# Modulation slices inside the wide stage, sums between products, first two wide chunks side by side

## The reference

```python
for l in range(DEPTH):                                   # DEPTH = 2
    mod_l = silu(c) @ w_mod[l] + b_mod[l]                # six vectors of 1024: sh1, sc1, g1, sh2, sc2, g2
    mod_c = silu(c_ctx) @ w_mod[l] + b_mod[l]            # the same for the context tokens
    y_l, y_c = token_mixer(modulate(rms_norm(x)), ...)   # retention, GLA, GQA, differential attention
    x = x + g1 * y_l
    x = x + g2 * conv_ffn(modulate(rms_norm(x, norm2[l]), sh2, sc2), w_up[l], conv_w[l], conv_b[l], w_down[l])
    # in layer 0 also for the context tokens

def conv_ffn(h, w_up, conv_w, conv_b, w_down):
    u = h @ w_up                                          # 1024 -> 2 x 2816
    a = depthwise_conv(u[..., :D_FF], conv_w, conv_b)     # width 3
    return (silu(a) * u[..., D_FF:]) @ w_down
```

## Time and profile before

| what | value |
|---|---|
| three timed runs | 2981.74, 2987.41, 2996.21 us; median 2987.41 us |
| the profiled execution | 2991.67 us, its span 2989.9 us |
| PE busy | 2731.8 us (91%) |
| POOL, DVE, ACT busy | 1522.0 us (51%), 1342.2 us (45%), 669.0 us (22%) |
| mean granted TensorE clock | 0.945 |
| DMA | 277.84 MB, mean 93 GB/s |
| wide stage of layer 0 | about 1142 to 1549 us |
| wide stage of layer 1 | from 2605 us |

### The profile page before, as it was taken

How to read it: one execution, slowest core, us unless ns; L and a number is a source line. 1 busy time by engine, 2 the same in 40 slices (tenths; PEclk the granted TensorE clock), 3 DMA queues, 4 the chain that set the end, 5 groups by cost and what they waited for, 6 DMA issues and landing times.

```text
span 2989.9 us, 37995 instructions
## 1 busy us (share of the span) xinstructions
PE 2731.8 (91%) x15620; PEld 2221.8 (74%) x15620; DVE 1342.2 (45%) x1756; ACT 669.0 (22%) x1130; POOL 1522.0 (51%) x1412
## 2 busy tenths in 40 slices
PE   5899989999988998999989997998889887899999
PEld 2688877777766886888877886786667666688877
DVE  4522066643566826555562135216643677421221
ACT  4211132221144511110020003013212245211110
POOL 2443447522412542565568524565834425488886
PEclk8899989999989998999989998999989898999999
DMA  7422412311311821333433362221212116333322
GB/s 244 134 66 89 116 31 62 87 38 50 106 38 40 256 72 57 113 113 113 121 103 111 91 205 55 83 68 49 65 50 61 46 36 208 88 92 98 94 89 80
DMA packets 361592, 277.84 MB, mean 93 GB/s; under 512 B 10139, under 2 KB 322111, under 8 KB 360908
## 3 DMA queue, kind: packets, MB, share of 16 engines
q1 hardware_dynamic: 359040, 272.57, 30.7%
q10 hardware_dynamic: 1612, 2.75, 0.2%
q0 software_dynamic: 768, 0.09, 0.0%
HBM read 246.01 MB, written 29.36 MB: 92 GB/s over the span
## 4 chain that ended last, share of the span: by engine, by line
PE 79%; DVE 11%; ACT 4%; POOL 3%; DMA 2%; issue 2%; SPq 0%; DVEq 0%; ACTq 0%; POOLq 0%
PE ps L445 18%; PE ps L446 17%; PE ps L447 17%; PE ps L664 4%; PE ps L990 3%; PE ps L595 2%; PE ps L484 2%; PE ps L486 2%; PE ps L485 2%; POOL w_hi L1127 1%; PE ps L684 1%; POOL w_lo L1130 1%; PE ps L626 1%; DVE arena L1695 1%; PE ps L791 1%
## 5 line engine op out<-in xcount | busy, mean ns | idle before, releaser
L1127 POOL TENSOR_TENSOR w_hi<-ring,tiny 128x512 fp32r<-128x512 f32 x516 | 592.2, 1148 | 1196.9 <-PE ps L447 659.5
L445 PE MATMUL ps<-hh,w_hi 128*128 128x512 f32 (+1 forms) x2272 | 852.6, 375 | 45.1 <-DVE hl L1665 24.7
L1130 POOL TENSOR_TENSOR w_lo<-ring,w_hi 128x512 fp32r<-128x512 f32 (+1 forms) x572 | 790.1, 1382 | 104.8 <-ACT w_hi L1291 64.4
L446 PE MATMUL ps<-hl,w_hi 128*128 128x512 f32 (+1 forms) x2272 | 826.2, 364 | 0.0
L447 PE MATMUL ps<-hh,w_lo 128*128 128x512 f32 (+1 forms) x2272 | 824.2, 363 | 0.0
L445 PEld LDWEIGHTS ps<-hh,w_hi 128*128 128x128 f32 x2272 | 446.4, 196 | 158.7 <-issue 56.9
L447 PEld LDWEIGHTS ps<-hh,w_lo 128*128 128x128 f32 x2272 | 445.2, 196 | 65.5
L446 PEld LDWEIGHTS ps<-hl,w_hi 128*128 128x128 f32 x2272 | 447.4, 197 | 60.2 <-issue 1.7
L1271 ACT ACTIVATE arena<-ps 128x512 f32<-128x512 f32 (+3 forms) x130 | 76.0, 584 | 442.2 <-PE ps L447 430.8
L484 PE MATMUL ps<-w_hi,hh 128*128 128x256 f32 (+1 forms) x544 | 157.6, 290 | 11.8 <-ACT arena L1271 11.8
L445 PE MATMUL ps<-ffh,w_hi 128*128 128x512 f32 x352 | 143.5, 408 | 19.2 <-POOL w_lo L1130 12.8
(11 more groups left out here) (242 smaller groups left out, 3849.7 us busy)
## 6 DMA issues: line engine op xcount, KB each, us to landing
ring<-in_w_in SPq DMA_DIRECT2D x118, 512.0 KB, 4.1
ring<-in_w_mod SPq DMA_DIRECT2D x96, 512.0 KB, 4.0
ring<-in_w_up SPq DMA_DIRECT2D x88, 512.0 KB, 4.3
ring<-in_w_down SPq DMA_DIRECT2D x48, 512.0 KB, 4.0
logits<-arena SPq DMA_DIRECT2D x32, 384.0 KB, 2.3
arena<-logits SPq DMA_DIRECT2D x32, 384.0 KB, 3.6
ring<-in_w_down SPq DMA_DIRECT2D x24, 384.0 KB, 3.4
ring<-in_w_branch SPq DMA_DIRECT2D x16, 512.0 KB, 4.5
```

Of the source, the lines that this page charges most:

```text
L445: pe.matmul(acc, wh[:, k], hi[:, n, x:y], start=n == 0, stop=False)
L446: pe.matmul(acc, wh[:, k], lo[:, n, x:y], start=False, stop=False)
L1127: pool.tensor_tensor(wh[:, 0:count], w, one[:].unsqueeze(2).to_broadcast([P, count, P]), ALU.mult).then_inc(*up("w_lead", ("lead", key, j)))
L1130: pool.tensor_tensor(wl[:, 0:count], w, wh[:, 0:count].bitcast(F32), ALU.subtract).then_inc(*up("w_split", ("split", key, j)))
```

## The change

The slices are spread by `n * 44 // 48` over the 44 up chunks, so that chunks 0, 11, 22 and 33 have two and the down stage has none, and DVE steps through them in the same places. The five sums inside the wide stage move into the second half of chunks 7, 14, 22, 29 and 36: after each tile of products (three matmuls) stand two of the sum's sixteen matmuls; before them PE waits for the last slice of the vector. The first two up chunks of either layer are done side by side: for each tile k first the products of chunk 0, then those of chunk 1; POOL splits the two in turns, half by half.

```diff
+def slices_with(l, c):
+    slices = next_modulation(l)
+    return [key for n, key in enumerate(slices) if n * 2 * FT // len(slices) == c]
+
+def vector_summed_with(c):
+    return {8 * (g + 1) * 2 * FT // 48: g for g in range(5)}.get(c)
...
         for c in range(2 * FT):
-            order += [("up", l, c)] + slices[c:c + 1]
+            order += [("up", l, c)] + slices_with(l, c)
         for n in range(3 * KT):
-            order += [("down", l, n // 3, n % 3)] + slices[2 * FT + n:2 * FT + n + 1]
+            order += [("down", l, n // 3, n % 3)]
...
+                        if summed is not None and j == 1:
+                            if x == 0:
+                                begin_sum(key[1] + 1, summed, (banks[0] + 4) % 8, (banks[0] + 4) % 8 + 1)
+                            for k in range(KT // 2):
+                                mm = product(acc[:, x:y], key, j, hi, lo, x, y, count=1, first=KT // 2 + k, offset=k)
+                                part_of_sum(key[1] + 1, summed, (KT // 2 if x else 0) + k)
...
+            def two_projections(keys, width, banks_of, each):
+                ends = segs(width)
+                for key, banks in zip(keys, banks_of):
+                    next_chunk(key)
+                    for s, n in room(key, *banks):
+                        pe.wait_ge(s, n)
+                for j in range(2):
+                    for key in keys:
+                        pe.wait_ge(*at(("split", key, j)))
+                    for k in range(KT // 2 * j, KT // 2 * (j + 1)):
+                        for key in keys:
+                            for x, y in ends:
+                                mm = product(psum(key)[:, x:y], key, j, hh, hl, x, y, count=1, first=k, offset=k - KT // 2 * j,
+                                             each=each if key == keys[0] and x == 0 else None)
+                            if k % (KT // 2) == KT // 2 - 1:
+                                mm.then_inc(*up("pe_half", ("half", key, j), *([("full", key)] if j else [])))
...
+            def begin_sum(l, g, *banks):
+                key = ("mods", l, g)
+                for s, n in room(key, *banks):
+                    pe.wait_ge(s, n)
+                base[key] = 512 * banks[-1] + 256
+                pe.wait_ge(*at(("used", ("slice", l, g, KT - 1))))
+
+            def part_of_sum(l, g, m):
+                key = ("mods", l, g)
+                for s in range(2):
+                    mm = pe.matmul(psum(key)[:, 2 * m + s:2 * m + s + 1], mod_sum[:, s, m * P:(m + 1) * P], one, start=True, stop=True)
+                if m == KT - 1:
+                    mm.then_inc(*up("pe_full", ("full", key)))
...
-                for c in range(2 * FT):
+                two_projections([("up", l, 0), ("up", l, 1)], W[l], [(0, 1), (2, 3)], lambda k: ("hl", l, 2, k))
+                for c in range(2, 2 * FT):
                     projection(("up", l, c), hh, hl, W[l], (2 * (c % 4), 2 * (c % 4) + 1),
-                               each=(lambda k: ("hl", l, 2, k)) if c == 0 else None)
-                    if l + 1 < DEPTH and c % KT == 0 and c > 0:
-                        sum_of_modulation(l + 1, c // KT - 1, 2 * ((c + 3) % 4), 2 * ((c + 3) % 4) + 1)
+                               summed=vector_summed_with(c) if l + 1 < DEPTH else None)
...
+                        pair = (0, 1) if first[0] == "up" and first[2] == 0 else (0,)
...
-                        modulation_step(l + 1, 2 * c // KT, 2 * c % KT)
+                    for key in slices_with(l, 2 * c):
+                        modulation_step(*key[1:])
...
-                for kind, n, g, k in next_modulation(l)[2 * FT:]:
-                    modulation_step(n, g, k)
```

More of the change, by code:

```diff
@@ L436, in next_chunk, with product @@
                 used[0] += 1
-            def product(acc, key, j, hi, lo, x, y, count=KT // 2, first=0, whole=KT, each=None):
+            def product(acc, key, j, hi, lo, x, y, count=KT // 2, first=0, whole=KT, each=None, offset=0):
                 wh, wl = w_halves(key, j)
@@ L444, in product, with projection @@
                         pe.wait_ge(*at(each(n)))
-                    pe.matmul(acc, wh[:, k], hi[:, n, x:y], start=n == 0, stop=False)
-                    pe.matmul(acc, wh[:, k], lo[:, n, x:y], start=False, stop=False)
-                    mm = pe.matmul(acc, wl[:, k], hi[:, n, x:y], start=False, stop=n == whole - 1)
+                    pe.matmul(acc, wh[:, offset + k], hi[:, n, x:y], start=n == 0, stop=False)
+                    pe.matmul(acc, wh[:, offset + k], lo[:, n, x:y], start=False, stop=False)
+                    mm = pe.matmul(acc, wl[:, offset + k], hi[:, n, x:y], start=False, stop=n == whole - 1)
                 return mm
-            def projection(key, hi, lo, width, banks, each=None):
+            def projection(key, hi, lo, width, banks, each=None, summed=None):
                 next_chunk(key)
@@ L459, in projection @@
                             pe.wait_ge(*at(("split", key, j)))
-                        mm = product(acc[:, x:y], key, j, hi, lo, x, y, first=KT // 2 * j,
-                                     each=each if each and (x == 0) == (each(0)[2] != "ctx") else None)
+                        if summed is not None and j == 1:
[4 more added lines that the diff above has]
+                                part_of_sum(key[1] + 1, summed, (KT // 2 if x else 0) + k)
+                        else:
+                            mm = product(acc[:, x:y], key, j, hi, lo, x, y, first=KT // 2 * j,
+                                         each=each if each and (x == 0) == (each(0)[2] != "ctx") else None)
                         if (x, y) == ends[-1]:
                             mm.then_inc(*up("pe_half", ("half", key, j), *([("full", key)] if j else [])))
+            def two_projections(keys, width, banks_of, each):
[14 more added lines that the diff above has]
+                                mm.then_inc(*up("pe_half", ("half", key, j), *([("full", key)] if j else [])))
             def token_projection(l, b, pair):
@@ L838, in turn_tokens @@
                 acc = psum(key)
+                src = xin
                 for t in range(NT):
@@ L841, in turn_tokens @@
                         pe.wait_ge(*at((kind + "_in", t)))
-                    mm = pe.transpose(acc[:, t * P:(t + 1) * P], xin[:, t, k * P:(k + 1) * P], ident)
+                    mm = pe.transpose(acc[:, t * P:(t + 1) * P], src[:, t, k * P:(k + 1) * P], ident)
                 mm.then_inc(*up("pe_full", ("full", key)))
@@ L1137, in split_until @@
                     first = split_chunks[done[0]]
-                    pair = next(p for p in token_pairs(first[2]) if first[3] in p) if first[0] == "t" else (0,)
+                    if first[0] == "t":
+                        pair = next(p for p in token_pairs(first[2]) if first[3] in p)
+                    else:
+                        pair = (0, 1) if first[0] == "up" and first[2] == 0 else (0,)
                     split(*split_chunks[done[0]:done[0] + len(pair)])
@@ L2032, in _ @@
                     step(right, "dve_free", ("free", key))
-                    if l + 1 < DEPTH:
-                        modulation_step(l + 1, 2 * c // KT, 2 * c % KT)
+                    for key in slices_with(l, 2 * c):
+                        modulation_step(*key[1:])
                     dve.wait_ge(*at(("silu", l, c)))
@@ L2038, in _ @@
                     dve.tensor_tensor(ff[:, c, 0:w], cu[:, 0:w], psum(key)[:, 0:w], ALU.mult).then_inc(*up("dve_free", ("free", key)))
-                    if l + 1 < DEPTH:
-                        modulation_step(l + 1, (2 * c + 1) // KT, (2 * c + 1) % KT)
+                    for key in slices_with(l, 2 * c + 1):
+                        modulation_step(*key[1:])
                 for c in range(FT):
```

## The result

The changed kernel took 3017.66 us (median of 8 runs), the kernel before 2993.99 us (median of 8 on the same chips): ratio 1.008, 95% interval 1.0064 to 1.0096, so it is slower by 0.8%, some 24 us. The forecast was 16.8 us slower. Its profiled execution spans 3013.7 us. The forecast time, 3004 us, was built on the 2987.41 us of the first three runs of the kernel before; with all eight that kernel's median is 6.6 us higher, so the two differences are what can be compared.

What follows compares the result with a forecast made beforehand. PE was taken to bound the kernel (79% of the chain), with its waits and clock. Lost 35.7, gained 18.9, net +16.8 us: 3004 us against the 2987.41 median; own range 2995 to 3014, stated range 2978 to 3022.

Steps and rivals of the forecast that it cites:

- Ring: Layer 0's wide stage: PE waits for late loads at chunks 12 and 34, 18.6 us lost together, and 24, 7.1 lost.
- Pair, layer 0: First two up chunks end 9.9 us sooner, but chunk 2 waits for its load: 4.3 us lost.
- Pair, layer 1: Start of layer 1's wide stage: no slices there, both chunks end sooner, 6.2 us gained.
- Sums: Five sums inside layer 0's wide stage: 7.6 us gained by mixing, 5.7 lost to stands of 2.87 at two chunks.
- The clock kept in the three without a stand: Mixed sums where PE does not wait for a slice: upper clock held, 2.2 us gained each.
- Lost in the two with: Mixed sums behind a stand, chunks 7 and 29: clock lost, 0.5 us gained each.
- Down stage: Layer 0, four slices gone: only 0.9 of the 7.8 us wait goes, column 1 follows at once, 5.1 us gained.
- POOL's ops beside the first down products back at 1.04 and 1.29: Sign expected in the profile after: POOL's ops there return to 1.04 and 1.29 us.
- R1: Rival, faster: loads of chunks 2, 12, 24 and 34 come in time, 2964 us; chance 0.1.
- R2: Rival, no change: mixed sums nearly free and the clock holds through them, 2986 us; chance 0.22.
- R3: Rival, slower still: clock falls in every mixed sum, POOL shut out of splits beside two slices, 3020 us; chance 0.18.

Runs made afterwards that it cites:

- the run with the shortened slice steps: Changed kernel's slice spreading alone, with the second DVE instruction left out of each slice step but a vector's first, result incomplete; 2998.26 us, one run.
- spread only: Changed kernel without the first two chunks side by side and with the sums as blocks behind their chunks; 3000.73 us, 1.0031 to the kernel before.
- four early: Changed kernel with first four slices behind out chunks 2 to 5, slice n behind up chunk n-4, sums in chunks 4, 12, 20, 28, 36; 2971.74 us, 0.9918.
- the run with block sums: Changed kernel with its five sums as blocks behind chunks 7, 14, 22, 29, 36, spread slices and pair kept; 2995.36 us, 1.0018 to the kernel before.
- sums in the context half: Changed kernel with the sum's sixteen matmuls four by four behind the context columns' tiles alone; 3001.29 us, 1.0035 to the kernel before.

## Why the forecast came out, step by step

- *Sign and size.* Slower, as forecast; 24 us where 16.8 were summed. The three stages that the edits touch make 27.7 in the trace, against 16.8. In the wide stage the terms were, forecast and measured: the start 4.3 and 4.9 lost, the ring 25.7 and 19.9 lost, the sums with their stands 1.9 gained and 13.8 lost. So one term was wrong by 15.7 us, and a too dear ring hid 5.9 of it: that the total lies within 11 us owes something to luck. The time itself, 3017.66 us, is above the forecast's own range (2995 to 3014) and inside the stated one.
- *Ring.* Right in place and cause, each wait about 2 us too long: 5.50, 5.50 and 3.65 us for 7.5, 7.5 and 5.3. All three terms of the sum were too large. At chunk 12, whose load waits for chunk 10 (full as chunk 11 begins), SP issued the load after 6.28 us for 7.05, because DVE's slice step took 2.48 us beside an idle POOL and not 3.55; from there POOL was on the chunk after 4.04 for 5.0; and its first pair of ops took 3.56 for 3.8:

```profile
1257.94 0.40 PE L456 MATMUL ps<-hh,w_hi 128*128 128x512 f32 x1
...
1261.71 2.48 DVE L1631 SCALAR_TENSOR_TENSOR rope<-ring,tiny,rope 128x1024 f32<-128x1024 f32 x2
...
1264.22 0.38 SPq L1114 DMA_DIRECT2D ring<-in_w_up  x1
...
1268.26 1.35 POOL L1179 TENSOR_TENSOR w_hi<-ring,tiny 128x512 fp32r<-128x512 f32 x1 [10.36 <-DMA ring<-in_w_up]
```

  The run with the shortened slice steps settled the cause.
- *Pair, layer 0.* PE entered chunk 2 31.2 us after the first product, before 28.5: 2.7 late, forecast 2.5, with a wait of 11.8 for "about 12". The gain was swallowed as the text said.
- *Pair, layer 1.* Right: chunk 2 begins 13.17 us after the first product where it began 18.82, so 5.65 gained for 6.2:

```profile
2624.05 0.39 PE L445 MATMUL ps<-hh,w_hi 128*128 128x512 f32 x1
```

```profile
2633.41 0.77 PE L456 MATMUL ps<-hh,w_hi 128*128 128x512 f32 x1 [6.65 <-DVE hl L1720]
...
2646.58 0.39 PE L456 MATMUL ps<-hh,w_hi 128*128 128x512 f32 x1
```

  The whole of layer 1 gained only 4.3, because the first column of its down stage took 21.5 us instead of 20.1; in spread only, without the pair, it took 21.5 too, in four early, with the pair, 20.1.
- *Sums, the step that failed.* "The clock kept in the three without a stand" held, as did the place of the two stands (3.88 and 2.97 us for 2.87). "Lost in the two with", at 1.7 us each, did not: the sum was taken to cost 4.7 behind a stand and cost 11.6, because the clock stays down as long as the mixture lasts, and its matmuls double too. That is 14 us, more than the whole miss. And loads do not hide in the mixture: 3.5 us for a forecast 2.96. The changed kernel's two stands with their sums cost 30 us; in the run with block sums the two sums cost 6.7 and 6.8, less than half.
- *Down stage.* 6.6 for 5.1, by another path: the forecast let the wait of 7.8 stand but for 0.9, and gave the chunk's arrival ahead of DVE's stream only as a bound. It did arrive ahead. The 7.8 and 2.27 for POOL went, but DVE's stream grew by 10.6 and PE waits 8.2 us for it instead of 4.2. The sign "POOL's ops beside the first down products back at 1.04 and 1.29" did not come: beside DVE's stream they took 1.4 to 1.6.
- *Rivals.* R1 is out: no load came in time. R2 and R3 each had half the truth: the mixed sums are cheap in three places and ruinous in two. The measured 3017.66 us is nearest R3's 3020, but by other terms: the clock did not fall in every mixed sum, and POOL was not shut out beside two slices (its ops took 2.0 to 2.2 us there).

## What to carry to other kernels

A ring shared by two kinds of loads gives each a lead by position: by the count of places, one extra entry takes a whole step of lead from the next two users, so count places before spreading work evenly. Small matmuls between large ones, two by two, kept a high clock high and a low clock low here, so nothing that can make TensorE stand belongs ahead of such a mixture. And test parts alone and together: here two parts gained 7 and 9 us alone, and beside the third the wide stage was 35.5 us longer than the three parts' own effects add up to.

## What the chip showed that was not expected

- *DVE and POOL, in turns or shut out.* Twenty-two DVE products with two inputs in SBUF shut one POOL op out for 12.77 us when it came 1.45 us after their start; when POOL began 0.38 or 0.60 us ahead, the two took turns: POOL 1.4 to 1.6 us an op, DVE 23.95 us for 13.33. "SBUF — State Buffer" of the Trainium skill (Who interferes with whom) says that issue order, not the shape of the op, decides who blocks. The traces agree for the op that starts ahead (behind POOL's, DVE's first product took 1.53 us for 0.68), but not for the whole stream. In sums in the context half POOL came 0.18 us after the stream's start and took turns. In the changed kernel it came back into the running stream after 1.75 us of idle time and was let in; in the kernel before, in layer 1, it had been ahead of the stream and was shut out when it came back later:

```profile
1590.35 1.51 POOL L1179 TENSOR_TENSOR w_hi<-ring,tiny 128x512 fp32r<-128x512 f32 x1 [1.75 <-PE ps L458]
```

```profile
2853.43 14.66 DVE L2043 TENSOR_TENSOR ffl<-arena,ffh 128x512 fp32r<-128x512 f32 x22
...
2859.63 9.37 POOL L1127 TENSOR_TENSOR w_hi<-ring,tiny 128x512 fp32r<-128x512 f32 x1 [4.12 <-PE ps L447]
```

  Over both layers of all fourteen traces, a POOL op that came at least one whole product into such a stream was shut out to its end (14 ops, 8.9 to 13.0 us) when POOL had been idle for 4.05 us or more, and let in (1.6 us at most) when it had been idle for 4.02 or less (all but one of them 3.1 or less). That is a pattern; what decides is open.
- *Weight loads follow the clock.* The sum's records stand 0.11 us apart at the upper level (0.44 for four) and 0.21 at the lower (0.85 for four). "TensorE: Matmul & The Clock Gate" of the Trainium skill (LDWEIGHTS) gives 107 ns for 128 columns without a clock; the trace agrees at the upper level alone.
